# Differential attention in a two-layer diffusion trunk: half of the value projection issued inside the attention loop, through one PSUM bank

## The reference

```python
q, k, v = jnp.split(h @ w_in, 3, axis=-1)          # h: normed tokens, 1024 wide
q = q.reshape(B, T, H, 2, d) * (d ** -0.5)
if rotate: q, k = _apply_rope(q, cos, sin), _apply_rope(k, cos, sin)   # latent tokens only
def attend(q, k, v):
    s = jnp.einsum('bqhjd,bshjd->bhjqs', q, k)
    p = jax.nn.softmax(s, axis=-1)
    a = p[:, :, 0] - lam_full * p[:, :, 1]
    o = jnp.einsum('bhqs,bshe->bqhe', a, v)
    return _rms(o) * subln_g * (1.0 - lam_init)
o_lat = attend(q_lat, k_all, v_all) @ w_out        # latents read all 512 tokens
o_ctx = attend(q_ctx, k_ctx, v_ctx) @ w_out        # context reads its own 256
```

## Time and profile before

| what | value |
|---|---|
| three runs without the profiler | 1889.65, 1889.93, 1890.08 us, median 1889.93 |
| the profiled execution | 1891.57 us, span of its instructions 1889.8 us |
| PE busy / weight loads | 1844.6 us (98%) / 1583.3 us (84%) |
| DVE, ACT, POOL busy | 1188.3, 688.1, 163.7 us |
| chain that ended last | PE 88%, DVE 7%, issue 2%, ACT 2% |
| granted TensorE clock, mean | 0.992 |

### The profile page before, as it was taken

The page is one execution under the profiler, slowest core; times in us unless marked ns, Lnnn a source line. Parts: engine busy times, 40 slices in busy tenths (PEclk is TensorE's granted clock), DMA queues, the critical chain, the costliest instruction groups (busy, mean ns, idle before and its releaser), DMA issues.

```text
span 1889.8 us, 27442 instructions
## 1 busy us (share of the span) xinstructions
PE 1844.6 (98%) x9984; PEld 1583.3 (84%) x9984; DVE 1188.3 (63%) x1890; ACT 688.1 (36%) x1152; POOL 163.7 (9%) x236
## 2 busy tenths in 40 slices
PE   8999999999989999999999999999998999989997
PEld 6888888898966888888889888888897899978886
DVE  7877772355478478777424787753358555667764
ACT  4332232232358242322223323222244333545542
POOL 0010100100301201001000110100102000010000
PEclk9999999999999999999999999999999999989998
DMA  8466643335420146656332566633343222545554
GB/s 322 151 205 196 193 153 108 93 104 161 134 67 1 67 134 209 191 189 189 96 105 90 178 211 189 199 119 92 94 142 123 68 88 90 191 144 186 191 167 124
DMA packets 81886, 271.85 MB, mean 144 GB/s; under 512 B 9489, under 2 KB 14865, under 8 KB 81809
## 3 DMA queue, kind: packets, MB, share of 16 engines
q1 hardware_dynamic: 62354, 201.58, 32.6%
q0 software_dynamic: 19456, 69.22, 12.3%
HBM read 267.62 MB, written 1.05 MB: 142 GB/s over the span
## 4 chain that ended last, share of the span: by engine, by line
PE 88%; DVE 7%; issue 2%; ACT 2%; DMA 0%; POOL 0%; SPq 0%; POOLq 0%; DVEq 0%; ACTq 0%
PE pt L1432 19%; PE pt L1433 19%; PE pt L1435 19%; PE pt L1407 9%; PE pt L1406 4%; PE pt L1627 2%; DVE wl L867 2%; PE pt L1842 2%; PE pt L1844 2%; PE pt L1843 2%; PE pt L1631 1%; PE pt L1505 1%; PE pt L1726 1%; PE pt L1727 1%; PE pt L1728 1%
## 5 line engine op out<-in xcount | busy, mean ns | idle before, releaser
L867 DVE TENSOR_TENSOR wl<-raw,wh 128x1024 fp32r<-128x1024 f32 (+2 forms) x394 | 435.7, 1145 | 410.9 <-ACT wh L578 407.0
L1432 PE MATMUL pt<-xh,wh 128*128 128x512 f32 (+1 forms) x1312 | 495.4, 378 | 0.2 <-DVE wl L867 0.2
L1433 PE MATMUL pt<-xh,wl 128*128 128x512 f32 (+1 forms) x1312 | 494.2, 377 | 0.0
L1435 PE MATMUL pt<-xl,wh 128*128 128x512 f32 (+1 forms) x1312 | 492.9, 377 | 0.0
L578 ACT CAST wh<-raw 128x1024 fp32r<-128x1024 f32 (+2 forms) x394 | 364.0, 970 | 273.3 <-PE pt L1435 148.9
L879 DVE CUSTOM_DVE_ANT_0 pt<-modw,raw 128x1024 f32<-128x1024 f32 x256 | 305.8, 1255 | 15.6 <-DMA modw<-in_mod_rows 15.5
L1432 PEld LDWEIGHTS pt<-xh,wh 128*128 128x128 f32 x1312 | 247.9, 189 | 45.3 <-issue 0.3
L1435 PEld LDWEIGHTS pt<-xl,wh 128*128 128x128 f32 x1312 | 247.7, 189 | 45.0
L1433 PEld LDWEIGHTS pt<-xh,wl 128*128 128x128 f32 x1312 | 247.8, 189 | 44.5
L727 ACT CAST uh<-tmp 128x512 f32 (+3 forms) x88 | 49.8, 568 | 291.9 <-DVE tmp L1171 283.4
L1432 PE MATMUL pt<-uh,wh 128*128 128x512 f32 x396 | 154.0, 389 | 0.0
(11 more groups left out here) (222 smaller groups left out, 2786.4 us busy)
## 6 DMA issues: line engine op xcount, KB each, us to landing
raw<-in_ffn_w SPq DMA_DIRECT2D x238, 512.0 KB, 4.0
modw<-in_mod_rows POOLq DMA_DIRECT2D x128, 512.0 KB, 4.6
raw<-in_ret_w_in SPq DMA_DIRECT2D x48, 512.0 KB, 4.4
raw<-in_diff_w_in SPq DMA_DIRECT2D x24, 512.0 KB, 4.4
raw<-in_ffn_w SPq DMA_DIRECT2D x32, 256.0 KB, 3.9
raw<-in_ret_w_out SPq DMA_DIRECT2D x16, 512.0 KB, 4.1
region<-in_mod_rows SPq DMA_DIRECT2D x8, 512.0 KB, 14.4
region<-in_mod_start SPq DMA_DIRECT2D x8, 512.0 KB, 15.0
```

Of the source, the lines that this page charges most:

```text
L867: nc.vector.tensor_tensor(flat(wl[:, s, cut]), raw[:, raw_slot(late, s, p), 0:part_rows * CW], flat(wh[:, s, cut].bitcast(F32)), ALU.subtr ...
L1432: nc.tensor.matmul(bank, w_hi[:, k, cut], hi(k), start=a, stop=False)
L1433: nc.tensor.matmul(bank, w_lo[:, k, cut], hi(k), start=False, stop=False)
L1435: return nc.tensor.matmul(bank, w_hi[:, k, cut], lo(k), start=False, stop=b)
```

## The change

Only the first pair of value chunks (columns 0 to 511, heads 0 to 3) stays in `diff_v`. The 192 matmuls of the second pair are issued inside the attention loop, in four quarters ("fills") of 48, all through PSUM bank 6: 12 matmuls in each of steps 1 to 4, 6 in each of steps 6 to 13, then 9, 6, 6, 6, 6, 6, 9 in steps 15 to 21 and the same in 23 to 29. ScalarE copies a finished quarter out at steps 5, 14, 22 and 30 (`filled`), and the next quarter waits for that copy. Bank 5 alone is left for head outputs, so `values` of head h waits for `scale_o` of head h-1. The steps of a head are moved: values at 4h+7 and 4h+8 (before 4h+6 and 4h+8), mean at 4h+9 (before 4h+10), scaling at 4h+10 (before 4h+11), turning, `hi_o` and `lo_o` at 4h+13 (before 4h+14).

The tokens are needed until the fills are done, so the finished heads go to `head_out`, which lies over `qk`. Queries and keys are rotated head by head (8 tiles in `diff_v`, 2 after the first row maximum, 6 at steps 6, 8, ..., 16), and POOL issues the copies of partner rows in four groups, each as soon as its four tiles exist. The splits of the weight chunks for the second value pair and the output projection move: steps 4, 15 and 32 on ScalarE, 4, 16 and 33 on VectorE.

```diff
-AT_SQUARE, AT_HI = TURN_LAG + 5, TURN_LAG + 10
-AT_MEAN, AT_SCALE, AT_LO = TURN_LAG + 6, TURN_LAG + 7, TURN_LAG + 10
-AT_TURN = TURN_LAG + 10
+AT_VALUES = (TURN_LAG + 3, TURN_LAG + 4)
+AT_SQUARE, AT_HI = TURN_LAG + 5, TURN_LAG + 9
+AT_MEAN, AT_SCALE, AT_LO = TURN_LAG + 5, TURN_LAG + 6, TURN_LAG + 9
+AT_TURN = TURN_LAG + 9
 V_STEPS = 4 * (DH - 1) + AT_HI + 1
+FILL = 2 * DT
+FILL_STEPS = ((1, (4, 4, 4, 4)), (6, (2,) * 8), (15, (3, 2, 2, 2, 2, 2, 3)), (23, (3, 2, 2, 2, 2, 2, 3)))
+AT_FILLED = {5: 0, 14: 1, 22: 2, 30: 3}
+AT_SPLIT, AT_REST = {4: (-1, 1), 15: (0, 0), 32: (0, 1)}, {4: (-1, 1), 16: (0, 0), 33: (0, 1)}
+ROPE_ORDER = [r for h in range(DH) for r in (h, DH + h)]
+ROPES_FIRST = 8
+AT_ROPE = {6 + 2 * n: ROPES_FIRST + 2 + n for n in range(6)}
...
+            head_out = sb("head_out", [P, 2 * DH, TOK], F32R, where=g)
...
-        other_rows = part(2 * DH, LAT, at=taken[0] - 2 * LAT - 2 * TT * LAT - 4 * TOK)
+        other_rows = part(2 * DH, LAT)
...
-                    for s in range(2):
-                        pool.wait_ge(evac[s], 2 * (ph["sa"], ph["sb"])[s])
                     n = DD // 4
                     for g in range(4):
+                        for s in range(2):
+                            pool.wait_ge(evac[s], 2 * ((ph["sa"], ph["sb"])[s] - 3 + g))
                         for b in range(P // n):
...
+                    def filled(f):
+                        s, b = divmod(f, 2)
+                        tile_done((values["sa"], values["sb"])[s] + 1, s, b, 2 * (values["q"] + 1) + s)
+                        nc.scalar.copy(vd[:, 2 * b:2 * b + 2, (2 + s) * CW:(3 + s) * CW],
+                                       pt[:, 6, :].rearrange("p (a c) -> p a c", a=2)).then_inc(evac[s], 1)
...
                     for v in range(V_STEPS):
+                        if AT_SQUARE <= v < AT_SQUARE + 4 * DH and (v - AT_SQUARE) % 4 == 0:
+                            square_o((v - AT_SQUARE) // 4)
                         if TURN_LAG <= v < V + TURN_LAG:
                             turn_out((v - TURN_LAG) // 2, (v - TURN_LAG) % 2)
                         if 0 < v < V:
                             exps(v // 2, v % 2)
-                        if v == 4:
-                            split(q0, 1, late=late)
...
+                        if v in AT_FILLED:
+                            filled(AT_FILLED[v])
+                        if v in AT_SPLIT:
+                            pair, s = AT_SPLIT[v]
+                            split(q0 + pair, s, late=late)
...
                     row_max(0, 0)
+                    rope(ROPES_FIRST)
+                    rope(ROPES_FIRST + 1)
                     row_max(0, 1)
...
-                        if v == 4:
-                            rest(2 * q0 + 1, 1)
+                        if v in AT_REST:
+                            pair, s = AT_REST[v]
+                            rest(2 * (q0 + pair) + s, s, late=late)
+                        if v in AT_ROPE:
+                            rope(AT_ROPE[v])
                         for at, step in ((AT_MEAN, mean_o), (AT_SCALE, scale_o), (AT_LO, lo_o)):
...
+                if g == 0 and b == 0:
+                    pe.wait_ge(roped, 2 * (h + 1))
...
+                    def fill(f, a, b):
+                        s, half = divmod(f, 2)
+                        if a == 0:
+                            if half == 0:
+                                pe.wait_ge(lo_ready, 2 * (2 * (before["q"] + 1) + s + 1))
+                            if f:
+                                was, t = divmod(f - 1, 2)
+                                pe.wait_ge(evac[was], 2 * ((before["sa"], before["sb"])[was] + 1) + t + 1)
+                        for i in range(a, b):
+                            n, k = 2 * half + i // DT, i % DT
+                            ins = value_products(pt[:, 6, (n % 2) * CW:(n % 2 + 1) * CW], s, n, k)
...
-                        if g == 0 and h >= 2:
-                            pe.wait_ge(o_scaled, h - 1)
+                        if g == 0 and h:
+                            pe.wait_ge(o_scaled, h)
...
                         if 0 < v < V:
                             score(v // 2, v % 2)
+                        fills(v)
                         if TURN_LAG <= v < V + TURN_LAG:
                             turn_probs((v - TURN_LAG) // 2, (v - TURN_LAG) % 2)
-                        if TURN_LAG + 2 <= v < V + TURN_LAG + 2 and (v - TURN_LAG) % 2 == 0:
-                            values((v - TURN_LAG) // 2 - 1)
+                        for g in range(2):
+                            if AT_VALUES[g] <= v < AT_VALUES[g] + 4 * DH and (v - AT_VALUES[g]) % 4 == 0:
+                                values(2 * ((v - AT_VALUES[g]) // 4) + g)
```

More of the change, by code:

```diff
@@ L213, in trunk @@
         with ExitStack() as g:
+            head_out = sb("head_out", [P, 2 * DH, TOK], F32R, where=g)
+        with ExitStack() as g:
             xn = sb("xn", [P, 2, TT, D], F32R, where=g)
@@ L1264, in _ @@
                         dve.wait_ge(evac[s], 2 * s0[s])
[L1265 to L1270 removed]
+                    for n in range(ROPES_FIRST):
+                        if n == ROPES_FIRST - 2:
+                            rest(2 * (q0 + 1), 0, late=late)
+                        rope(n)
                 elif kind == "diff_attn":
```

110 lines of the change are left out of this document (53 added, 57 removed).

## The result

| | before | changed kernel |
|---|---|---|
| median of the runs, us | 1889.85 (1889.65 to 1890.08) | 1920.99 (1919.28 to 1922.06) |
| the profiled execution, us | 1891.57 | 1922.06 (span 1920.4) |
| mean granted clock | 0.992 | 0.982 |

The ratio is 1.0162, 95% interval 1.0149 to 1.0176: 31 us slower. The direction was forecast, the size was not: +15.3 was forecast, and 1920.99 lies outside the range of 1896 to 1911.

What follows compares the result with a forecast made beforehand. PE, busy 98%, bounds the kernel. From 518.4, 64 + 23 us of work plus waits of 4.0 (entry), 17.5 (turns) and some 6 (tail) give 633.2, +15.3 us: 1889.9 becomes 1905; range 1896 to 1911.

Steps and rivals of the forecast that it cites:

- Entry and projection: Half the projection, 23.0 us, moves into the loop, entered at 518.4 in place of 541.5; gain at most 12 us.
- Rotations and transfers: Eight rotations take 9 us of VectorE inside the loop; partner-row transfers start earlier; PE cost 0 to 0.5 us.
- Entry wait at step 6: PE waits 3.6 us for ScalarE's copy of the first fill quarter; first values start at 537.0.
- One bank: Values wait for the previous head's scaling: a turn is 13.4 us against 11.2 of PE work, 2.2 us waited.
- six waits of 2 to 4.5 us: Sign of being right: six such PE waits before the latent values, released by VectorE's scaling.
- Copies at steps 14 and 22 hidden: ScalarE's copies of later fill quarters end about 12 us after a scaling, inside PE's waits for the scaling.
- Tail: After head 5's scaling, 8.7 us to head 7's values, then 2.8 us to the output projection at 633.2.
- The clock: PE waits of 3.6 and 4.5 us might lower the clock; one drop costs 1.7 us; taken as 0, range 0 to 3.4.
- only the structural part of the wait: Rival: ScalarE's exponentials and the mix are early, so a turn waits 1.0 us, not 2.2; 1897 us; chance 0.15.
- PE is fed: Rival: scaling ends before PE arrives, so a turn is PE's 11.2 us; 1878 to 1885, say 1882; chance 0.08.
- weight-load view: Rival: only weight loads cost PE, so 33.7 us are free and 23.0 vanish whole; 1867 us; chance 0.02.
- Slower still: Rival: longer hand-offs or records, 0.5 us a turn, plus 1.7 us for the clock; 1910 us; chance 0.13.

Runs made afterwards that it cites:

- e9: The changed kernel with idle zero products on PE ahead of the scaling waits at heads 1, 3, 5, 7 and ahead of the second fill quarter; 1913.25 us.
- e13: The changed kernel with idle zero products ahead of every long wait of PE in the loop; 1909.51 us.
- e4: The changed kernel with VectorE's order turned: mean first in its step, scaling behind the first mix; 1908.17 us.
- e5: The kernel before with one bank for head outputs, moved steps, no fills, and 14 idle products ahead of waits for the scaling (6 for the last head); 1918.42 us.
- e2: The kernel before with all head outputs in bank 5 and the steps of a head moved, no fills; 1924.59 us.
- e3: The kernel before with only the steps of a head moved as in the change, two banks, no fills; 1896.89 us.
- e14: The kernel before with only the latent values one step later, at 4h+7 in place of 4h+6; 1899.46 us.
- e8: The changed kernel with later fills in halves ahead of the values, mean first and scaling behind the first mix on VectorE, and weight casts moved; 1900.01 us.
- e15: The kernel before with only the normalisation one step earlier and squares first in their step on ScalarE, values in their old place; 1891.57 us.

## Why the prediction was wrong in size

- *Entry and projection.* Right: 517.95 for 518.4.
- *Rotations and transfers.* Right as far as seen: none of PE's waits in the list from 490 to 660 ends in a rotation or a transfer.
- *Entry wait at step 6.* Right: 3.49 us for 3.6, ended by the copy of a fill (L807). But the work behind it took 5.0 us (534.57 to 539.59) in place of 2.6. In e9, at clock 1.00, it takes 2.8 (534.46 to 537.26), so 2.2 us are the clock's first cost, in the window 534 to 538 at 0.50.
- *One bank.* The mechanism and its length were right: turns of 14.0, 14.9, 15.8, 14.1 and 13.6 us in e13 for 13.9, 14.5, 15.7, 13.4 and 13.4, and a sixth of 14.0 for 13.8 from scaling to scaling. The sign "six waits of 2 to 4.5 us" came out as four, at heads 1, 3, 5 and 6, each within 0.3 us of the walk. The expectation that ratio, mix, mean and remainder lie on the chain is supported by e4: taking most of them off it took 7.8 us off those waits.
- *Copies at steps 14 and 22 hidden.* Wrong in a small way: PE waits for them 1.63 us (567.52) and 1.53 (601.07), one step ahead of the values of heads 2 and 4, which then wait no more. At full clock those turns had nearly the forecast length all the same (14.9 and 14.1 in e13 for 14.5 and 13.4); but each wait opens a stretch of low clock.
- *Tail.* The walk was right: 8.7 and 2.6 us in e13 for 8.7 and 2.8; the changed kernel took 10.8 and 5.1.
- ***The clock*: the step that failed.** I wrote "One drop costs 2 x 2 x 0.43 = 1.7 us of work, and part of that would lie in waits; I take 0 and keep 0 to 3.4 in the range." Three things in it were wrong. I priced a drop once, while there are as many as there are turns. I took the 4.9 us wait of the earlier trace rows as the case, and the attention window at 1.00, whose longest gap is 2.37 us, as a sign that shorter ones are safe, while in the changed kernel waits of 1.53, 1.63, 1.99, 2.54 and 2.58 us are each followed by a window of 2 us at 0.50. And I assumed that part of the loss hides in waits, while what runs slowly is the work right behind a wait: values, score, fill, transposes, the head of the next turn's chain, so nearly all of it counts. What is missing from the sum is 2.6 us at the entry and 0.4, 1.8, 0.5, 3.4, 1.0, 1.8, 2.1 and 2.3 in the turns, 15.9 together; the slow work read off the trace is 16.3 and is spread in the same way, except that in two turns (1-2 and 6-7) 0.7 to 1.0 us of it was hidden. Of the 15.9 e13 wins back 11.5 with idle products, though they cost something themselves (2.8 in one turn). For the other 4.4 no run shows that they come back at full clock.

The Trainium skill (TensorE: Matmul & The Clock Gate, Why this matters for your kernels) says that idle gaps between bursts of matmuls bring the clock down; I cited it and then gave it 2 to 3 us. The trace agrees, at shorter gaps and far more often than I allowed: e5 against e2 is the price in a clean loop, 1.5 us a head over four heads.

The rivals: "only the structural part of the wait" and "PE is fed" were both wrong, since the waits at heads 1, 3, 5 and 6 have the forecast length. The weight-load view (1867) was wrong by 54 us. "Slower still" named the right place, the clock, and gave it 1.7 us in place of 16. The moved steps, which I costed at nothing, cost 7 to 9 us in a loop with two banks (e3, e14); in the changed kernel this lies inside the turns, whose length was walked through with the steps at their new places, so it is no separate term of the sum.

## What to carry to other kernels

A wait on PE can cost more than its length: in this loop nearly every wait of 1.5 us or more was followed by work at half speed. Price the work right behind it so, above all where it heads the chain to the next wait, and count one such drop per round of the loop. A second buffer for an accumulator may be worth more than all the holes that giving it up would fill; walk the chain from release to release before trading it. When a kernel shows such drops, a few idle products ahead of the wait are a cheap test (here 31 us of loss became 19). Placed behind another wait they only delay the work. Shortening the waits themselves did more here: 31 us of loss became 9 in e8.

## What the runs showed that I had not expected

- The same wait may or may not bring the clock down. The kernel before has a gap of 2.37 us at 543 and stays at 1.00; e15, which is identical up to that point, has the same gap and then:

```profile
545.02 0.70 PE L1507 MATMUL pt<-region 64*128 64x256 f32 x4 [2.37 <-ACT region L606]
545.93 2.08 PE L1507 MATMUL pt<-region 64*128 64x512 f32 x4 [0.21 <-ACT modw L606]
```

and, in its windows:

```profile
546.00:548.00 2.00, 2.00 (x5) 0.50 (x5) 1.47 (x3) 1.02 (x4) 0.00 (x0) 0.50 0.00 0
```

  e3 and e14 show 0.51 and 0.50 there too. One profile at 1.00 is no proof that a gap is harmless.
- Moving 16 products by one step of the four that a head takes cost 9.2 us over 8 heads, with every instruction the same (e14).
- Products of zeros with zeros hold the clock as well as real ones: 1.00 over 580 to 604 in e5, where the same loop without them has 0.79.
